# Two transformer blocks in one kernel: mLSTM steps a piece earlier, squares and splits moved, products of zeros at the start

## The reference

```
h = num / max(|den|, exp(-m_t))
h = h * rsqrt(mean(h * h) + eps)
```

## Time and profile before

| | us |
|---|---|
| median of three runs (2512.10 to 2512.36) | 2512.27 |
| the profiled execution | 2515.16 |
| its span | 2513.10 |
| PE busy | 2480.9 |
| DVE busy | 1746.5 |
| ACT busy | 1280.9 |
| DMA engines, mean busy share | 56% |
| first work of ACT, POOL and SP in the span | 0.75, 0.24, 0.75 |
| first product on PE | 7.20 |

### The profile page before, as it was taken

How to read it: one execution, slowest core, us unless ns; L and a number is a source line. 1 busy time by engine, 2 the same in 40 slices (tenths; PEclk the granted TensorE clock), 3 DMA queues, 4 the chain that set the end, 5 groups by cost and what they waited for, 6 DMA issues and landing times.

```text
span 2513.1 us, 38835 instructions
## 1 busy us (share of the span) xinstructions
PE 2480.9 (99%) x15416; PEld 2217.6 (88%) x15416; DVE 1746.5 (69%) x2277; ACT 1280.9 (51%) x1630; POOL 36.9 (1%) x35
## 2 busy tenths in 40 slices
PE   8999999999999999999999999999999999999999
PEld 8999998888888888888888888889988888888887
DVE  7998597765876578787678766664875565665665
ACT  5345565544554455655555444454544444444454
POOL 0000100000000000100000000001000000000001
PEclk9999999999999999999999999999999999999999
DMA  8565546555555555555555566655465555555552
GB/s 271 168 187 175 195 152 200 184 188 193 177 194 188 193 187 184 168 171 166 158 176 168 168 185 186 191 192 189 161 201 188 189 194 186 185 190 192 186 185 101
DMA packets 304530, 459.34 MB, mean 183 GB/s; under 512 B 11408, under 2 KB 152976, under 8 KB 304400
## 3 DMA queue, kind: packets, MB, share of 16 engines
q1 hardware_dynamic: 304256, 457.39, 56.1%
q10 hardware_dynamic: 144, 0.13, 0.0%
HBM read 455.39 MB, written 2.10 MB: 182 GB/s over the span
## 4 chain that ended last, share of the span: by engine, by line
PE 83%; DVE 2%; ACT 1%; issue 1%; DVEq 0%; ACTq 0%
PE ps L682 26%; PE ps L680 23%; PE ps L683 13%; PE ps L679 11%; PE ps L690 2%; PE ps L688 2%; PE ps L689 2%; PE ps L784 1%; PE ps L782 1%; DVE w_split L1747 1%; ACT w_split L1141 0%; PE ps L785 0%; PE ps L781 0%; PE ps L724 0%; PE ps L728 0%
## 5 line engine op out<-in xcount | busy, mean ns | idle before, releaser
L1747 DVE TENSOR_TENSOR w_split<-raw,w_split 128x1024 fp32r<-128x1024 f32 (+1 forms) x857 | 1046.0, 1223 | 714.3 <-ACT w_split L1141 712.7
L1141 ACT ACTIVATE w_split<-raw 128x1024 fp32r<-128x1024 f32 x855 | 902.8, 1059 | 1024.8 <-PE ps L680 810.1
L682 PE MATMUL ps<-h_split,w_split 128*128 128x512 f32 x1818 | 712.9, 398 | 0.7 <-DVE scaled L1747 0.5
L680 PE MATMUL ps<-h_split,w_split 128*128 128x512 f32 x1590 | 630.2, 396 | 0.0
L683 PE MATMUL ps<-h_split,w_split 128*128 128x256 f32 x1818 | 505.7, 278 | 0.0
L679 PE MATMUL ps<-h_split,w_split 128*128 128x256 f32 x1590 | 443.6, 279 | 0.0
L683 PEld LDWEIGHTS ps<-h_split,w_split 128*128 128x128 f32 x1818 | 342.6, 188 | 68.0
L682 PE MATMUL ps<-act_split,w_split 128*128 128x512 f32 x1004 | 391.0, 396 | 0.4 <-DVE scaled L1747 0.3
L679 PEld LDWEIGHTS ps<-h_split,w_split 128*128 128x128 f32 x1590 | 299.0, 188 | 72.7
L682 PEld LDWEIGHTS ps<-h_split,w_split 128*128 128x128 f32 x1818 | 345.4, 190 | 12.9 <-DVE w_split L1747 1.5
L680 PE MATMUL ps<-act_split,w_split 128*128 128x512 f32 x868 | 343.5, 396 | 0.0
(11 more groups left out here) (305 smaller groups left out, 2961.6 us busy)
## 6 DMA issues: line engine op xcount, KB each, us to landing
raw<-w_up SPq DMA_DIRECT2D x152, 1024.0 KB, 5.1
raw<-w_in SPq DMA_DIRECT2D x114, 1024.0 KB, 5.2
raw<-w_down SPq DMA_DIRECT2D x108, 1024.0 KB, 5.0
raw<-w_out SPq DMA_DIRECT2D x32, 1024.0 KB, 5.0
raw<-w_in SPq DMA_DIRECT2D x18, 512.0 KB, 5.0
raw<-w_branch_m SPq DMA_DIRECT2D x8, 1024.0 KB, 5.3
raw<-w_branch_a SPq DMA_DIRECT2D x8, 1024.0 KB, 5.3
outT<-x SPq DMA_DIRECT2D x8, 256.0 KB, 2.5
```

Source lines behind the costliest of these rows:

```text
L680: last = nc.tensor.matmul(wide, hi[:, cols], rhs[:, k, :], start=False, stop=end)
L682: nc.tensor.matmul(wide, hi[:, cols], rhs[:, k, :], start=first, stop=False)
L1141: nc.scalar.activation(split_home(n)[0], raw[:, slot, half:half + 1024], ACT.Copy).then_inc(hi_ready, 1)
L1747: return nc.vector.tensor_tensor(out, a, b, op)
```

## The change

1. TensorE begins with seven float32 products of zeros (128x128 by 128x256, into bank 3), behind a memset of `val_b[:, 0, :]` on DVE and ahead of its credit for `piece_used`.
2. ACT's first activation is Sqrt instead of Copy. Squares 6 and 7 of the first norm come behind the split of piece 7, before the wait for `small_loaded`; so do DVE's sums 1 to 5. Sums 6 and 7 with the fold stay behind piece 8.
3. mLSTM: on ACT the squares go from r = 14 to 13 and the scaled copy from 16 to 15; on DVE the denominator goes from 13 to 12 and the factor from 15 to 14.
4. `BOUNDARY_SPLITS` is a table for each norm. At N_PRE2 splits 6 and 7 both come at pair 5, on DVE before that pair's low halves. The other two norms keep their places.
5. Chunk 3 of the second w_in waits for a pair one earlier (`after` = 2).
6. The first residual product comes before the wait for the last squares; the fifth comes with the others, not behind the first product of y. The fifth output part is sent by ACT, not by SP.

```diff
-        M_PE, M_ACT, M_DVE = (4, 9, 14), (8, 14, 16, 19), (7, 9, 13, 15, 18, 20)
+        M_PE, M_ACT, M_DVE = (4, 9, 14), (8, 13, 15, 19), (7, 9, 12, 14, 18, 20)
-        BOUNDARY_SPLITS = {3: 5, 5: 6, 6: 7}
+        BOUNDARY_SPLITS = {N_PREF1: {3: (5,), 5: (6,), 6: (7,)}, N_PRE2: {3: (5,), 5: (6, 7)},
+                           N_PREF2: {3: (5,), 5: (6,), 6: (7,)}}
...
-            for q in (0, 1, 2, 5, 3, 6, 4, 7):
+            for q in (0, 1, 2, 5, 3, 6, 7):
...
                 last_piece(norm, n.plus(pieces - 1), pieces - 1, rhs)
+                if norm == N_POSTF2:
+                    pe.wait_ge(x_settled, 24)
+                    residual(0)
                 pe.wait_ge(pair_folded, POST[norm] + 1)
...
+            pe.wait_ge(warm_cleared, 1)
+            for i in range(WARM):
+                nc.tensor.matmul(ps[:, 3, 0:T], val_b[:, 0, 0:128], val_b[:, 0, :], start=True, stop=True)
             pe.sem_inc(piece_used, USED_CREDIT)
...
-                after = 2 if c == 2 else 1
+                after = 2 if c < 4 else 1
...
-            for q in range(4):
+            for q in range(1, 5):
                 residual(q)
             for q, bank in SUMMED_PAIRS.items():
                 pe.wait_ge(y_scaled, q + 1)
-                if q == 1:
-                    residual(4)
...
-            nc.scalar.activation(root[:, 0:1], glu[:, 0, 0:1], ACT.Copy).then_inc(copy_loaded, 1)
+            nc.scalar.activation(root[:, 0:1], glu[:, 0, 0:1], ACT.Sqrt).then_inc(copy_loaded, 1)
...
+            for q in (6, 7):
+                square_pre(N_PRE1, q)
             act.wait_ge(small_loaded, 32)
...
-                if n == 8:
-                    square_pre(N_PRE1, 6)
-                    square_pre(N_PRE1, 7)
...
+            act.wait_ge(sum_taken, 5)
+            act.dma_start(outT[:, 8:10, :], x[:, 8:10, :]).then_inc(stored, 16)
...
+            nc.vector.memset(val_b[:, 0, :], 0.0).then_inc(warm_cleared, 1)
...
+            add_squares(N_PRE1, 1, 2, 3, 4, 5)
             dve.wait_ge(small_loaded, 32)
...
                 if n == 8:
-                    add_squares(N_PRE1, 1, 2, 3)
-                elif n == 9:
-                    add_squares(N_PRE1, 4, 5, 6, 7)
+                    add_squares(N_PRE1, 6, 7)
...
+                    splits = BOUNDARY_SPLITS[pre].get(q, ())
                     if q < 7:
                         weigh(2 * q + 2, 2)
+                    if len(splits) > 1:
+                        for p in splits:
+                            split(Step(next_piece + p))
```

More of the change, by code:

```diff
@@ L260, in build @@
         cleared = sem("cleared")
+        warm_cleared = sem("warm_cleared")
         squares_ready = sem("squares_ready")
@@ L392, in build @@
         GATE_COLUMNS, SCALE_COLUMN = 19, 11
-        BOUNDARY_SPLITS = {3: 5, 5: 6, 6: 7}
+        BOUNDARY_SPLITS = {N_PREF1: {3: (5,), 5: (6,), 6: (7,)}, N_PRE2: {3: (5,), 5: (6, 7)},
+                           N_PREF2: {3: (5,), 5: (6,), 6: (7,)}}
         SUM_BANK = {N_PRE1: 7, N_PREF1: 2, N_PRE2: 7, N_PREF2: 2}
         GAINED = 6
+        WARM = 7
         SUMMED_PAIRS = {0: 7, 1: 1, 2: 2, 3: 3, 4: 6}
@@ L805, in sum_norm, with residual @@
                 sum_channels([square_sum[:, 0, :]], SUM_BANK[norm], stat_summed)
+            def residual(q):
+                nc.tensor.matmul(ps[:, SUMMED_PAIRS[q], :], identity,
+                                 x[:, 2 * q:2 * q + 2, :].rearrange("p a t -> p (a t)"), start=True, stop=False)
             def closing_chunk(norm, n, rhs, pieces, taken):
@@ L1292, in first_mixer @@
             def first_mixer(n):
-                if n == 8:
-                    square_pre(N_PRE1, 6)
-                    square_pre(N_PRE1, 7)
-                elif n == 11:
+                if n == 11:
                     act.wait_ge(copy_loaded, 1)
@@ L1379, in post_and_pre @@
                 for q in range(8):
-                    if q in BOUNDARY_SPLITS:
-                        split(Step(next_piece + BOUNDARY_SPLITS[q]))
+                    for p in BOUNDARY_SPLITS[pre].get(q, ()):
+                        split(Step(next_piece + p))
                     high_pair(pre, gain, q, x_ready, 16 * POST[post] + 2 * q + 1)
@@ L2106, in post_and_pre @@
                         add_y(post, y, post_gain, 2 * q + 2, 2)
-                    if q in BOUNDARY_SPLITS:
-                        split(Step(next_piece + BOUNDARY_SPLITS[q]))
+                    if len(splits) == 1:
+                        split(Step(next_piece + splits[0]))
                 make_floor(post)
```

## The result

| | before | after |
|---|---|---|
| median of five executions each | 2512.36 (2512.10 to 2515.06) | 2499.17 (2498.77 to 2499.53) |
| ratio, 95% interval | | 0.9943 [0.9933, 0.9954] |
| profiled execution, its span | 2515.16, 2513.10 | 2499.27, 2497.30 |
| granted clock over the span | 0.997 | 0.998 |

The kernel is 13.2 us faster. I had said 16.5 and 2495.8, with 2493.0 to 2501.5 as the range: in the range, on its upper side, 3.4 us above the point and outside the forecast's own 2494 to 2497.5.

What follows compares the result with a forecast made beforehand. TensorE is busy 99% of the span, so only its waits and low-clock stretches can be won: 5.5 + 2.3 + 8.1 + 0.6 = 16.5 us, from the median 2512.27 to 2495.8 us, range 2493 to 2501.5.

Steps and rivals of the forecast that it cites:

- Start and squares: Kernel start and first norm: products of zeros plus earlier squares and sums save 5.5 us (bounds 3.2 and 5.5).
- The 0.65: Start: of 2.0 us won by the full clock only 0.65 arrives, as the second piece waits for DVE's low half.
- Boundary: Second block's opening: the 1.78 us split wait and low clock go, 3.4 us, of which 2.3 stays (bounds 1.7 and 3.9).
- the 0.56 of slack: Behind the second block's opening: the piece needing DVE's split started 0.56 us after it; 1.78 + 0.56 gives 2.3.
- mLSTM: mLSTM transposes: waits of 1.54 twice, 2.35 at head 1 and 2.7 of low clock go: 8.1 us (bounds 3.1, 8.7).
- rival 2: mLSTM head 1: ACT's order is worse than laid out, wait and clock fall stay, keeping 5.0 us: 2500.8; chance 0.15.
- its drain: ACT at head 1: the skill's 1.4 us drain per table load would add 2.8 us of wait; the trace showed none.
- End: Kernel end: earlier residual product and one output transfer ahead of the queue save 0.6 us (bounds 0.1 and 0.8).
- the basis: Whole kernel: 16.5 us of terms from the profiled execution subtracted from the median 2512.27, 2.9 us below the profiled one.
- rival 1: Clock falls at other waits, 1.6 to 2.7 us each: 2498 to 2502; chance 0.25, a fifth of it for falls landing anew.
- a sign of being wrong: Anywhere: the clock falls at a wait that it kept before, or a wait over 1.5 us stands before a transpose.
- Rivals 3 and 4: Start: zeros do not lift the clock, 2496.4, chance 0.07; or zeros leave it low, slower than before, chance 0.03.

Runs made afterwards that it cites:

- only_start: Kernel before the change with only the products of zeros and the earlier first-norm squares and sums (items 1 and 2): median 2508.99 us, ratio 0.9982.
- only_mlstm: Kernel before the change with only the mLSTM steps a piece earlier (item 3): median 2505.99 us, ratio 0.9972.
- only_tail: Kernel before the change with only the new end (item 6: residual products, fifth output part on ACT): median 2512.72 us, ratio 0.9998.
- fill_no_mlstm: fill with the mLSTM steps on ACT and DVE put back where they were before the change: median 2505.24 us.
- fill: The changed kernel plus two float32 products of constants in the wait at each of the three norm openings: median 2497.85 us.
- after_again: The changed kernel timed once more in the second session, nothing altered: median 2499.33 us, ratio 0.9949 to the kernel before.
- only_boundary: Kernel before the change with only the second block's splits moved and chunk 3's looser count (items 4 and 5): median 2510.49 us, ratio 0.9993.

## Why the prediction was nearly right, and where it was off

**Start and squares: 5.5 forecast, 6.1 measured** (312.67 and 306.56). Opening 1 scatters by 0.7 us among kernels with the same start, 312.01 to 312.68 and 306.31 to 307.07; by the means of these it is 5.8. The sum's wait went whole and the clock stayed up, both as worked out. The 0.65 was too small: I held DVE's low half of the second piece at its time of before, 10.25, by the landing of its block. That landing isn't fixed: ACT started on the block at 9.16 in before, and between 8.36 and 9.06 in the profiled executions of the thirteen other kernels, with products of zeros and without. The second piece then began at 10.85, not at 11.5, behind a wait of 0.15 us instead of 1.4. In the eight executions with the products of zeros and the earlier squares, opening 1 follows this start by 297.95 to 298.09 us, late or early as it comes.

**Boundary: 2.3 forecast, 2.1 measured**, by the way from opening 2 to the first product of chunk 4: 1113.72 - 1057.56 = 56.16 and 1106.25 - 1052.20 = 54.05. The waits handed back are where I put them: 0.38 behind the sum, 0.81 about 24 us later. What I missed is that the 0.56 of slack was itself made by the low clock, which held TensorE back. From opening 2 to head 0's transposes, its own wait taken off, before needs 100.0 us, only_start and only_mlstm, which have the 1.78 but no fall, 98.4, and after 97.8. So against an execution that kept its clock the part gives 0.6, and the other 1.6 is the fall.

**mLSTM: 8.1 forecast, 8.6 measured** (1780.33 - 1113.72 = 666.61 against 1764.30 - 1106.25 = 658.05). Heads 0 and 2 lost their waits, head 1 kept 0.62 where I had 0.6. ACT's order came out as laid out, and rival 2 fell. Of its drain nothing is to be seen: the next activation begins 1.30 us after a load of 1.28 began. The Trainium skill (ScalarE: Activation LUTs, What ACT_TABLE_LOAD costs) has the drain behind each load; this trace does not agree.

**End: 0.6 forecast, 0.8 measured**, the upper bound (732.8 and 732.0 in before and only_tail).

**What failed: the basis and rival 1.** The terms alone give 16.5, the stages 6.1 + 2.1 + 8.6 + 0.8 = 17.6. Of these, 0.8 and 1.0 were lost again by falls at openings 1 and 3 (745.6 for 744.8; 733.0 for 732.0): 15.8, the difference of the two spans. Between the medians 13.2 are left. The step that failed is "The median of the runs is 2.9 us below the profiled one, so 2512.27 - 16.5". I subtracted terms that hold for the profiled execution from a median of others, as if 2.9 us were the profiler's. It was not: that execution had more low clock. Of 47 executions of before in the three sessions of experiments, the 26 whose granted clock was 0.999 took 2511.7 us on average, 11 at 0.998 took 2513.4, 9 at 0.997 took 2514.5, one at 0.996 took 2516.5. The typical execution had less to win than the one I read. Where its clock was low is not seen, as only one of each kernel was profiled; by the profiled ones of other kernels it can be, with the boundary's fall absent, 1.6 less; with a shorter one behind head 1, about 1.2 less (2.9 us there in before, 1.7 in fill_no_mlstm, by the way from head 1 to head 2, head 2's wait taken off). That is 2.8; the terms that were 1.1 too small made up for part of it, which is luck. So fill, which has no fall, is at 2497.85, 2.0 above the forecast, and after's falls add the other 1.3.

Rival 1 happened, in the form to which I gave a fifth of its quarter: falls land anew in each execution. It is also what the prediction named as a sign of being wrong: the clock fell at waits that it had kept. I counted them in the profiled executions, by the wait in front:

| wait, us | times in these executions | clock fell behind it |
|---|---|---|
| 1.54 (heads 0, 2) | 10 | 0 |
| 1.78 (boundary) | 5 | 3 |
| 2.1 to 2.2 (openings, unfilled) | 21 | 5 |
| 2.9 (head 1) | 5 | 5 |
| 2.1 to 3.9 (first sum) | 5 | 5 |

The same wait, opening 1 in after and after_again, had a fall in one execution and none in the next. Length orders the chances but does not decide: the first sum's wait of 2.1 us in only_tail had its fall, and of the six executions of fill_no_mlstm, which has the 2.9, one had a granted clock of 1.000. The Trainium skill (TensorE: Matmul & The Clock Gate, Part 1) says that the monitor runs free and is not reset when a kernel starts; the traces agree with it. I set the rule aside because three executions lay within 0.26 us. The next two were 2513.33 and 2515.06. Rival 1's price was too high for the places where falls came: 0.8 and 1.0 us at the openings, against 1.6 to 2.7. Rivals 3 and 4 fell: the first real products ran at full clock in after.

## What to carry to other kernels

A profiled execution is one draw. Before subtracting terms of its trace from a median, look at its granted clock beside that of the others, and count a fall of the clock by its chance, not as part of the wait's price. Removing waits pays twice where they are the long ones (9 of 9 profiled waits of 2.7 us and more here had a fall behind them), and a wait that can't be removed can be filled with constant products: 1.5 us for six products in all. Where two parts feed the same wait, they don't add up: opening 1 came at 312.67 with neither, at 312.06 with the earlier products alone (within the scatter), at 308.98 with the earlier sums alone, and at 306.56 with both.

## What was not expected of the hardware

- Products of zeros raise the granted clock as those of data do: seven of them, from 1.20 to 5.9, and the first real product at 7.57 ran at the full clock, 1.68 us later.
- Nothing but constant products in three waits of 2.1 to 2.2 us took a spread of 2498.56 to 2500.06 down to 2497.30 to 2498.16. What scatter stays goes with the landing of the second weight block, behind which ACT starts on it at 8.4 to 9.1.
- The clock can fall late: behind the 2.12 us wait of after, TensorE did 1.3 us of products at full clock before it went low for 3.4 us (307.86 to 311.28). In only_boundary it fell with the first product behind the same wait (312.73), and in before it fell at 1210.01, 0.8 us before the wait at head 1 ended.
